# Hybrid encoder on one core: masks moved between the levels, prompt rows loaded a unit sooner, query preparation in two parts, another order at the experts' ends

## Chip, cores and metric

The kernel runs on one core of one Trainium2 chip. The metric is the device time of one execution in microseconds; lower is better.

## What is computed

One encoder layer is applied to two groups with the same weights: a prompt of 512 tokens and a sample of 1024 tokens, each of width 1024. The layer is a mixer (four differential-attention heads and four bidirectional HGRN2 heads of width 128, from one common input projection, then an output projection) and an expert-choice feed-forward (16 experts, each takes the 2/16 of a group's tokens that score highest), with norms ahead of both and at the end. Cut to the core:

```python
def trunk(x):
    x = x + mixer(rms_norm(x, norm_mix_g))
    x = x + expert_choice_ffn(rms_norm(x, norm_ffn_g))
    return rms_norm(x, final_norm_g)

def mixer(h):
    aq, ak, av, hq, hff, hfb, hi, hg = split(h @ w_in)
    att = diff_attention(aq, ak, av, lam)          # softmax(q1 k1) - lam * softmax(q2 k2), distance bias
    att = rms_norm(att, subln_g) * (1 - lam_init)
    o_f = hgrn2_chunk_scan(silu(hq), 1 - f_f, hi, log(f_f))       # forward
    o_b = flip(hgrn2_chunk_scan(flip(...), 1 - f_b, ...))         # backward
    hgo = rms_norm(o_f + o_b, hg_norm_g) * silu(hg)
    return concat(att, hgo) @ w_out

def expert_choice_ffn(h):
    g, idx = top_k(softmax(h @ w_router).T, cap)   # cap: 128 of the sample, 64 of the prompt
    hid = silu(xs @ w_gate) * (xs @ w_up)          # xs = h[idx]
    return scatter_add(idx, (hid @ w_down) * g)
```

## The kernel before, in words

Activations and weights are split into a high and a low part (`w_hi` by a cast on ScalarE, `w_lo` by a subtraction on VectorE), and each product is three matmuls (hi*hi, lo*hi, hi*lo; L599 to L601). Each engine runs its own program; steps are named by tuples, and every engine walks through the same written list of steps. Semaphores (`Signal`, counted by head and number) tie the engines together.

The order of the program is this, with the times of the profiled execution. First the sample's and the prompt's rows are normalised and turned (0 to 30 us). The turned prompt rows go to DRAM and come back later. Then come the sample's four hgrn heads: a first head, a loop, and a last one "joined" with the first projection units of attention (345 to 425). Then the sample's attention heads: three in a loop-like form (425 to 650, the last of them called lone), and the last one, the "crossing" (650 to 727), in whose gaps the first units of the prompt's hgrn head stand. Then the prompt's hgrn heads (730 to 865), its joined head (865 to 910), its attention heads (910 to 1007), the output projection with router and choice of tokens (1007 to 1226), and the experts (1229 to 2143), an ending behind them.

- `Projection` (L510) multiplies input-projection weights of one head with the rows. Its work comes in units, a unit in `CUTS` pieces. VectorE's `split_lo` (L572) makes `w_lo`, ScalarE's `split_hi` (L568) `w_hi`. `summed` counts PE's finished pieces.
- `unpack` (L475) brings the prompt's turned rows back from DRAM in four quarters: SP's load into `hP_raw` (L486), ScalarE's cast into `hP_hi` (L492), VectorE's subtraction into `hP_lo` (L500). The rows of the sample lie in the same memory, so SP waits until the sample's last projection is done.
- `hgrn` (L845) works in blocks of 512 tokens (two for the sample, one for the prompt: 12 blocks in all). In a block each of seven "levels" multiplies decayed queries and keys (VectorE L1130 to L1141, PE L997 to L1008) into the PSUM banks `X[0..3]`. Step `diag` takes from each bank the 12 x 32 numbers of the diagonal with a mask (L1181) and sums the 12 (L1186); GpSimd places the result (L1276). Then follow the state (L1203) and the normalised output (L1216), turned by PE at L1056.
- `attention` (L1293) works in tiles of 128 queries. Scores (L1449, L1450), two custom operations and exponentials (L1581, L1528), the state of weights (L1598), a turn by PE (L1463), the product with v (L1472) and the output. After four tiles the output is normalised (L1620), turned (L1480) and written to `mixT` (L1627, step `mix`). Step `take` prepares the next head's keys and queries: ScalarE L1517 and L1521, VectorE L1568. Turned keys go through ScalarE to `k_rows` (L1535).
- `project_out` (L1649) runs over tiles of 128 tokens; L1815 is the router product, L1822 and L1829 turn its scores.
- The experts work on units of 128 rows of weights; `gather` fetches the chosen rows (GpSimd L2420), `turn` transposes them on PE (L2187, L2188), ScalarE L2251 and VectorE L2326 split them to `x_parts`; `split` is L2244 and L2319 for weights; units are L2210 and L2212. The ending adds the last expert (L2378, L2383, L2390), and normalises and scatters the last rows (L2369, L2460).

## Time and profile before

| | us |
| --- | --- |
| median of three runs | 2164.92 |
| lowest and highest | 2163.8, 2165.94 |
| the profiled execution | 2165.15 |
| its span in the trace | 2162.9 |
| mean granted TensorE clock | 0.973 |

| engine | busy us | share of the span |
| --- | --- | --- |
| PE | 1996.9 | 92% |
| DVE (VectorE) | 1450.8 | 67% |
| ACT (ScalarE) | 1108.7 | 51% |
| POOL (GpSimd) | 352.6 | 16% |

PE is TensorE, PEld its weight load. A wait row names the instruction that waited and the one that released it. The span is shorter than the time of the execution by what lies before the first and behind the last instruction. L numbers are lines of the kernel before; in the changed kernel the same lines stand some 6 to 30 lines further down (L1181 becomes L1193, L2187 becomes L2215).

### The profile page before, as it was taken

What the parts mean: (1) busy time and instruction counts of PE and PEld (TensorE: products, weight loads), DVE (VectorE), ACT (ScalarE), POOL (GpSimd) and SP (SyncE); (2) the same over time, 40 slices, a digit from 0 to 9 for tenths busy, and PEclk for the clock granted to TensorE, in tenths of its full rate; (3) what the DMA queues carried; (4) which work ended last, traced back from release to release, by engine and by line L of the source; (5) the groups of instructions that cost most, each with busy time, mean ns of one, the idle gap of its engine ahead of it and who ended that gap; (6) DMA issues with size and microseconds to landing.
All of it is one profiled execution on the core that took longest, in us unless ns stands there. A gap on an engine that the chain in (4) does not pass through costs nothing. (4 is left out here: it accounts for less than half of the span.)

```text
span 2162.9 us, 43529 instructions
## 1 busy us (share of the span) xinstructions
PE 1996.9 (92%) x16048; PEld 1746.7 (81%) x16048; DVE 1450.8 (67%) x2601; ACT 1108.7 (51%) x1983; POOL 352.6 (16%) x587
## 2 busy tenths in 40 slices
PE   7999998899998998888899199999999999999996
PEld 6877876788787776677788199999999999999995
DVE  5366575666667666676258677777777777778875
ACT  5322322465566433366222066667666766667774
POOL 1213213000000122201221001111111111111233
PEclk9999999999999999999999599999999999999998
DMA  5211100100002222112232278777878887778995
GB/s 183 84 31 32 35 27 17 41 18 24 20 6 88 64 58 82 62 52 80 98 117 100 109 231 265 247 260 247 266 246 260 247 263 248 259 257 297 345 323 189
DMA packets 183465, 317.82 MB, mean 147 GB/s; under 512 B 11872, under 2 KB 82016, under 8 KB 183328
## 3 DMA queue, kind: packets, MB, share of 16 engines
q1 hardware_dynamic: 169984, 281.06, 38.5%
q0 software_dynamic: 8608, 30.68, 5.7%
q10 hardware_dynamic: 4736, 4.19, 0.7%
q8 instruction: 93, 1.52, 0.3%
q14 instruction: 44, 0.36, 0.1%
HBM read 279.97 MB, written 35.91 MB: 146 GB/s over the span
## 5 line engine op out<-in xcount | busy, mean ns | idle before, releaser
L2319 DVE TENSOR_TENSOR we_lo<-raw,we_hi 128x1024 fp32r<-128x1024 f32 x384 | 465.9, 1223 | 189.2 <-ACT we_hi L2244 188.4
L2210 PE MATMUL psum<-x_parts,we_hi 128*128 128x384 f32 x2048 | 585.5, 360 | 3.1 <-DVE we_lo L2319 3.1
L2212 PE MATMUL psum<-x_parts,we_lo 128*128 128x192 f32 x2048 | 513.6, 251 | 0.0
L2244 ACT CAST we_hi<-raw 128x1024 fp32r<-128x1024 f32 x384 | 400.1, 1054 | 157.0 <-PE psum L2212 93.7
L2212 PEld LDWEIGHTS psum<-x_parts,we_lo 128*128 128x128 f32 x2048 | 392.3, 192 | 0.6
L2210 PEld LDWEIGHTS psum<-x_parts,we_hi 128*128 128x128 f32 x2048 | 385.8, 188 | 4.1 <-issue 3.5
L599 PE MATMUL psum<-hT_hi,w_hi 128*128 128x512 f32 x512 | 213.8, 417 | 1.4 <-issue 0.7
L601 PE MATMUL psum<-hT_hi,w_lo 128*128 128x512 f32 x512 | 201.7, 394 | 0.0
L600 PE MATMUL psum<-hT_lo,w_hi 128*128 128x512 f32 x512 | 201.4, 393 | 0.0
L599 PE MATMUL psum<-hP_hi,w_hi 128*128 128x512 f32 x256 | 109.8, 429 | 16.5 <-DVE w_lo L572 12.2
L134 POOL TENSOR_TENSOR carried_pool<-minus_half 128x1 f32<-128x1 f32 x47 | 16.9, 359 | 635.3 <-ACT result_s L2286 489.6
L601 PEld LDWEIGHTS psum<-hT_hi,w_lo 128*128 128x128 f32 x512 | 97.0, 189 | 21.6
L599 PEld LDWEIGHTS psum<-hT_hi,w_hi 128*128 128x128 f32 x512 | 97.0, 189 | 21.1 <-DVE w_lo L572 1.3
L600 PEld LDWEIGHTS psum<-hT_lo,w_hi 128*128 128x128 f32 x512 | 97.3, 190 | 16.3
L572 DVE TENSOR_TENSOR w_lo<-w_raw,w_hi 128x512 fp32r<-128x512 f32 x96 | 68.1, 709 | 56.5 <-ACT w_hi L568 54.8
L600 PE MATMUL psum<-hP_lo,w_hi 128*128 128x512 f32 x256 | 102.3, 400 | 0.0
L601 PE MATMUL psum<-hP_hi,w_lo 128*128 128x512 f32 x256 | 102.0, 398 | 0.0
L2226 PE MATMUL psum<-we_hi,hid_parts 128*128 128x512 f32 x256 | 101.3, 396 | 0.0
L2227 PE MATMUL psum<-we_lo,hid_parts 128*128 128x512 f32 x256 | 99.8, 390 | 0.0
L2228 PE MATMUL psum<-we_hi,hid_parts 128*128 128x512 f32 x256 | 99.7, 390 | 0.0
L2230 PE MATMUL psum<-we_lo,hid_parts 128*128 128x512 f32 x256 | 99.6, 389 | 0.0
L2229 PE MATMUL psum<-we_hi,hid_parts 128*128 128x512 f32 x256 | 99.6, 389 | 0.0
(313 smaller groups left out, 3836.2 us busy)
## 6 DMA issues: line engine op xcount, KB each, us to landing
raw<-in_w_gate SPq DMA_DIRECT2D x128, 512.0 KB, 4.7
raw<-in_w_up SPq DMA_DIRECT2D x128, 512.0 KB, 6.9
raw<-in_w_down SPq DMA_DIRECT2D x128, 512.0 KB, 5.0
w_raw<-in_w_in SPq DMA_DIRECT2D x96, 256.0 KB, 2.8
y_rows<-x SPq DMA_DIRECT2D x12, 512.0 KB, 2.6
h_rows<-h SPq DMA_DIRECT2D x12, 512.0 KB, 2.9
y<-y_rows SPq DMA_DIRECT2D x12, 512.0 KB, 8.0
w_raw_s<-in_w_in SPq DMA_DIRECT2D x16, 256.0 KB, 3.1
```

The source lines that it names most:

```text
L599: pe.matmul(out[:], mem.w_hi[:, u % 2, n, :], hi, start=(k == 0), stop=False)
L600: pe.matmul(out[:], mem.w_hi[:, u % 2, n, :], lo, start=False, stop=False)
L601: mm = pe.matmul(out[:], mem.w_lo[:, u % 2, n, :], hi, start=False, stop=(k == DT - 1))
L2210: pe.matmul(out[:, 0:2 * SLOTS], w_hi[:, s, at], x_parts[p][:, k, :, :], start=(k == 0), stop=False, skip_group_check=True)
L2212: mm = pe.matmul(out[:, SLOTS:2 * SLOTS], w_lo[:, s, at], x_hi[p][:, k, :], start=False, stop=(k == DT - 1), skip_group_check=True)
L2226: pe.matmul(out[2 + h][:], a, u, start=first, stop=False)
L2227: pe.matmul(out[2 + h][:], a, v, start=False, stop=False)
L2228: pe.matmul(out[2 + h][:], b, u, start=False, stop=last)
L2229: pe.matmul(out[h][:], both, u, start=first, stop=False)
L2230: mm = pe.matmul(out[h][:], both, v, start=False, stop=last)
L2244: act.copy(w_hi[:, n % PARTS, :], raw[:, s, :]).then_inc(hi.sem, 1)
L2319: dve.tensor_tensor(w_lo[:, n % PARTS, :], raw[:, n % RAW, :], w_hi[:, n % PARTS, :].bitcast(F32), ALU.subtract).then_inc(lo.sem, 1)
```

## The change

Seven parts:

1. **Masks inside the levels.** `diag` no longer reads the banks. One of the four masks stands behind level 5 and three behind level 6, and they write to rows of 32 with the four banks side by side. `diag` is then four additions over 768, 384, 128 and 128 elements, each on the result of the one before, in place of four reductions.
2. **Prompt rows a unit sooner.** `unpack` waits for attention's next-to-last unit of the last sample head instead of its last. The memory is cut anew, so that the raw rows and the early half don't lie on what the last unit reads. Two quarters are unpacked in the lone head, two in the crossing; only the late half waits for the last unit. PE's own wait at the start of the prompt's hgrn (`start`) is gone.
3. **Queries in two parts.** `take` 0 makes both keys and the first pair of queries, `take` 1 the second pair a tile later.
4. **Output turn a tile later.** `mix` of the first half stands at tile 6 between two pieces instead of behind tile 5.
5. **Dummy matmuls.** PE multiplies `ident` with itself 16 times behind the router product of the next-to-last tile, and 28 times ahead of the experts' first turn.
6. **Experts' start.** The first three weight splits stand ahead of the first turn, and SP lets the gathered rows land before it issues the fourth weight chunk.
7. **Experts' end.** The last expert's prompt rows are added, normalised and scattered ahead of the sample's rows.

```diff
+def keep_clock(pe, bank, ident, count):
+    for _ in range(count):
+        pe.matmul(bank[:, 0:P], ident[:], ident[:], start=True, stop=True)
...
+        {"hP_raw": ([P, DT, TP], F32), "hP_late": ([P, 2, HALF, TP], F32R), "hP_early": ([P, 2, HALF, TP], F32R),
+         "w_raw_p": ([P, 2, HALF, P], F32)},
...
-        sp.wait_ge(before.proj.summed.sem, before.proj.summed.last(HEADS - 1))
+        sp.wait_ge(summed.sem, summed.at(HEADS - 1, before.proj.NB * (before.proj.units - 1) - 1))
...
+            if 2 * q >= HALF:
+                act.wait_ge(summed.sem, summed.last(HEADS - 1))
+            act.copy(half_of(0, q), of(mem.hT_raw, q)).then_inc(hi_done.sem, 1)
...
+    in_lone = {("norm", 1): [step for _, step in unpacked[0:2]]}
...
+    at_step = {("scores", 0, 0): [("h", ("split", 0))], ("exp", 1, 0): unpacked[2:3], ("weigh", 0): unpacked[3:4]}
...
-            elif kind == "start":
-                all_mixed(pe)
...
+        behind_level = {5: (0,), 6: (1, 2, 3)}
...
+                for n in behind_level.get(k, ()):
+                    dve.wait_ge(placed.sem, placed.at(i, 4 * b - 1))
+                    dve.tensor_tensor(mem.masked[:, :, n, :], X[n][:, 0:12 * 32].rearrange("p (k t) -> p k t", t=32),
+                                      mem.masks[:], ALU.mult).then_inc(masked.sem, 1)
...
-                for n in range(BC):
-                    e = BC * b + n
-                    dve.wait_ge(summed_up.sem, summed_up.at(i, e - 2))
-                    dve.tensor_tensor(mem.masked[:, n % 2, :, :], X[n][:, 0:12 * 32].rearrange("p (k t) -> p k t", t=32),
-                                      mem.masks[:], ALU.mult).then_inc(masked.sem, 1)
-                    dve.wait_ge(masked.sem, masked.at(i, e))
-                    if n == 0:
-                        dve.wait_ge(placed.sem, placed.at(i, 4 * b - 1))
-                    dve.tensor_reduce(mem.diag[:, n, :], mem.masked[:, n % 2, :, :].rearrange("p k t -> p t k"),
-                                      AX_X, ALU.add).then_inc(summed_up.sem, 1)
+                dve.wait_ge(masked.sem, masked.at(i, BC * b + BC - 1))
+                for e, (to, of) in enumerate(((slice(0, 6), slice(6, 12)), (slice(0, 3), slice(3, 6)),
+                                              (slice(0, 1), slice(1, 2)), (slice(0, 1), slice(2, 3)))):
+                    dve.wait_ge(summed_up.sem, summed_up.at(i, 4 * b + e - 1))
+                    dve.tensor_tensor(mem.masked[:, to, :, :], mem.masked[:, to, :, :], mem.masked[:, of, :, :],
+                                      ALU.add).then_inc(summed_up.sem, 1)
...
+        if turned_out:
+            slots += [("piece", CUTS * (t + 1)), ("mix", t // BC - 1)]
         if 0 < t < NT:
             slots.append(("weigh", t))
         if t == NT - 1:
-            slots.append(("take",))
-        if t < NT - 2 + NB:
+            slots.append(("take", 0))
+        if turned_out:
+            slots.append(("piece", CUTS * (t + 1) + 1))
+        elif t < NT - 2 + NB:
             slots.append(("pieces", t + 1))
         elif NB == 2:
-            slots.append(("pieces", NT + 1))
+            slots += [("take", 1), ("pieces", NT + 1)]
         else:
-            slots.append(("piece", CUTS * NT + t - NT + 1))
-        if middle:
-            slots.append(("mix", t // BC - 1))
...
+                m = step[1]
+                if m == 0:
+                    act.wait_ge(proj.land_act.sem, proj.land_act.at(j, NB * K + NB - 1))
+                    if i is None:
+                        for held in (before.signals[name] for name in ("mixed", "o_summed", "gates", "gate_taken")):
+                            act.wait_ge(held.sem, held.last(HEADS - 1))
+                    act.wait_ge(scored.sem, scored.last(j - 1))
+                    for of in range(2):
+                        act.copy(k_both[of][rows_of(of), 0:T], mem.land[K][rows_of(of), 0:T]).then_inc(k_first.sem, 1)
+                for half in range(2):
+                    high = act.activation(q_hi[m][rows_of(half), 0:T], mem.land[Q][rows_of(m), 0:T], ACT.Copy,
+                                          scale=slope_cols[rows_of(m), 0, bass.ds(j, 1)])
...
+                if t == NT - 2:
+                    pe.wait_ge(added, 2 * (NT - 1))
+                    keep_clock(pe, SUMS[NT % 2][0], ident, 16)
...
             body("gather", 0, 0)
+            for n in range(PARTS - 1):
+                body("split", 0, 0, n)
             body("turn", 0, 0)
             body("gather", 0, 1)
-            for n in range(PARTS - 1):
-                body("split", 0, 0, n)
...
+                            if p == 0 and n == PARTS - 1:
+                                sp.wait_ge(gathered.sem, gathered.at(0, 31))
...
+                    if kind == "gather":
+                        if p == 0:
+                            keep_clock(pe, half(p, "gate")[0], ident, 28)
+                    elif kind == "turn":
...
+        in_turn = sorted(when, key=lambda q: when[q]) + [NT + 2 * LATE - 1, NT + 2 * LATE - 2]
```

The order of instructions is shown at three places, register instructions left out. VectorE, at the first block of a sample's hgrn head, the last level's operands (`q`, `k`) and the diagonal. Before (L572 weight split, L1181 mask, L1186 sum, L1130 the state's operands):

```order
L1139 TENSOR_TENSOR q1<-q1,fup 128x4x64
L1141 TENSOR_TENSOR k1<-k1,fup 128x4x64
L572 TENSOR_TENSOR w_lo<-w_raw_s,w_hi 128x512
L1181 TENSOR_TENSOR table<-psum,table 128x384
L1186 TENSOR_REDUCE table<-table 128x32
L1181 TENSOR_TENSOR table<-psum,table 128x384
L1186 TENSOR_REDUCE table<-table 128x32
L1181 TENSOR_TENSOR table<-psum,table 128x384
L1186 TENSOR_REDUCE table<-table 128x32
L1181 TENSOR_TENSOR table<-psum,table 128x384
L1186 TENSOR_REDUCE table<-table 128x32
L1130 TENSOR_TENSOR q0<-q0,f10 128x512
```

After (L1193 is the mask, L1201 an addition, L1154 and L1156 the operands, L586 the split):

```order
L1156 TENSOR_TENSOR k1<-k1,fup 128x8x32
L1193 TENSOR_TENSOR table<-psum,table 128x12x32 x3
L1154 TENSOR_TENSOR q0<-q0,fup 128x4x64
L1156 TENSOR_TENSOR k0<-k0,fup 128x4x64
L1154 TENSOR_TENSOR q1<-q1,fup 128x4x64
L1156 TENSOR_TENSOR k1<-k1,fup 128x4x64
L586 TENSOR_TENSOR w_lo<-w_raw_s,w_hi 128x512
L1201 TENSOR_TENSOR table<-table 128x768
L1201 TENSOR_TENSOR table<-table 128x384
L1201 TENSOR_TENSOR table<-table 128x128
L1201 TENSOR_TENSOR table<-table 128x128
L1145 TENSOR_TENSOR q0<-q0,f10 128x512
```

The masks moved ahead of the last level's operands (one stands two pairs of rows further up, behind level 5) and of the weight split; the four reductions are gone and four shorter additions stand behind the split.

ScalarE, at the crossing, from the last `take` of the sample to the first exponentials of its last head. Before:

```order
L1517 CAST k_both<-land 64x1024 x2
L1521 ACTIVATE q_hi<-land,slope_cols 64x1024 x4
L568 CAST w_hi<-w_raw 128x512
L1535 COPY k_rows<-psum 128x512 x2
L1541 ACTIVATE squares,small<-psum 128x128 x4
L1504 COPY land<-psum 128x512 x2
L1528 ACTIVATE q,small<-k,small 128x1024 x2
L1509 COPY v_rows<-psum 128x512 x2
L1528 ACTIVATE f,small<-k,small 128x1024
L492 CAST hP_hi<-hP_raw 128x1024 x2
L568 CAST w_hi<-w_raw 128x512
L492 CAST hP_hi<-hP_raw 128x1024 x2
```

After (L1536 and L1538 are `take`, L582 the weight cast, L1552 k_rows, L506 the prompt rows):

```order
L1536 CAST k_both<-land 64x1024 x2
L1538 ACTIVATE q_hi<-land,slope_cols 64x1024 x2
L582 CAST w_hi<-w_raw 128x512
L1552 COPY k_rows<-psum 128x512 x2
L1538 ACTIVATE q_hi<-land,slope_cols 64x1024 x2
L1558 ACTIVATE squares,small<-psum 128x128 x4
L506 CAST hP_early<-hP_raw 128x1024 x2
L1521 COPY land<-psum 128x512 x2
L582 CAST w_hi<-w_raw 128x512
L1545 ACTIVATE q,small<-k,small 128x1024 x2
L1526 COPY v_rows<-psum 128x512 x2
L1545 ACTIVATE f,small<-k,small 128x1024
L506 CAST hP_late<-hP_raw 128x1024 x2
```

Two of the four query rows moved behind the k_rows copies; the first two casts of prompt rows moved ahead of the copies of the projection, in front of the last head's exponentials.

PE, from the output projection's last product of the sample's second-last tile to the experts' first turn. Before (L1794 product, L1815 router, L1822 and L1829 turns of scores, L2187 and L2188 turns of gathered rows):

```order
L1794 MATMUL psum<-wo,w_lo 128x512
L1815 MATMUL psum<-router,h2T 128x16 x8
L1822 MATMUL psum<-ident,small_o 16x128
L1804 MATMUL psum<-ident,h_1 128x128 x8
L1815 MATMUL psum<-router,h2T 128x16 x8
L1822 MATMUL psum<-ident,small_o 16x128
L1829 MATMUL psum<-ident,merging 128x16 x4
L2187 MATMUL psum<-ident,rows_p 128x128
L2188 MATMUL psum<-ident,rows_s 128x128
```

After (L140 is the dummy, L1814 the product, L1835 the router, L1845 and L1852 the turns of scores, L2215 and L2216 those of rows):

```order
L1814 MATMUL psum<-wo_hi,w_lo 128x512
L1835 MATMUL psum<-router,h2T 128x16 x8
L140 MATMUL psum<-ident 128x128 x16
L1845 MATMUL psum<-ident,small_o 16x128
L1824 MATMUL psum<-ident,h_1 128x128 x8
L1835 MATMUL psum<-router,h2T 128x16 x8
L1845 MATMUL psum<-ident,small_o 16x128
L1852 MATMUL psum<-ident,merging 128x16 x4
L140 MATMUL psum<-ident 128x128 x28
L2215 MATMUL psum<-ident,rows_p 128x128
L2216 MATMUL psum<-ident,rows_s 128x128
```

Sixteen dummies now stand ahead of the wait for the scores, and 28 ahead of the first turn. On ScalarE and VectorE the first three weight splits moved ahead of this turn's copies.

## Rows read from the trace of the kernel before

**Rows 1.** The page's first line; windows (length, busy us of each engine).

```profile
span 2162.9 us, 43529 instructions
...
1246.00:2143.00 897.00, 895.00 (x5552) 843.24 (x5552) 660.34 (x859) 599.37 (x915) 153.32 (x167) 1.00 0.81 266
```

**Rows 2.** PE's waits in the whole span (total us, times, longest).

```profile
PE psum L1829 <- DVE merging L1969: 23.9, 2, 14.1
...
PE psum L599 <- DVE w_lo L572: 12.8, 12, 7.9
...
PE psum L1463 <- DVE mixT L1627: 2.7, 4, 0.7
```

**Rows 3.** The same, 30 to 345 us, then 345 to 425 us.

```profile
PE psum L997 <- DVE table L1181: 4.9, 6, 1.0
...
PE psum L997 <- DVE table L1181: 3.3, 4, 1.1
```

**Rows 4.** Groups by line (ns), then groups of the page.

```profile
L1181 DVE TENSOR_TENSOR table<-psum,table x48: 539/550/559, 113.7 to 891.6; 128x384 f32<-128x384 f32 x48
...
L1186 DVE TENSOR_REDUCE table<-table x48: 803/850/881, 114.3 to 892.2; 128x32 f32<-128x384 f32 x48
...
L2319 DVE TENSOR_TENSOR we_lo<-raw,we_hi 128x1024 fp32r<-128x1024 f32 x384 | 465.9, 1223 | 189.2 <-ACT we_hi L2244 188.4
...
L572 DVE TENSOR_TENSOR w_lo<-w_raw,w_hi 128x512 fp32r<-128x512 f32 x96 | 68.1, 709 | 56.5 <-ACT w_hi L568 54.8
```

**Rows 5.** What PE waited for in 865 to 910 us.

```profile
PE psum L1056 <- DVE normed L1216: 3.3, 1, 3.3
```

**Rows 6.** Timeline, the crossing (start, length, [idle before <-releaser]).

```profile
660.41 1.28 DVE L1598 SCALAR_TENSOR_TENSOR state<-q,small 128x1024 f32<-128x1024 f32 x1
...
663.49 0.79 PE L599 MATMUL psum<-hP_hi,w_hi 128*128 128x512 f32 x1 [7.86 <-DVE w_lo L572]
...
668.13 0.27 PE L1463 MATMUL psum<-ident,state 128*128 128x128 f32 x1
```

**Rows 7.** Timeline at the start of the prompt's hgrn heads.

```profile
730.37 0.49 PE L599 MATMUL psum<-hP_hi,w_hi 128*128 128x512 f32 x1 [1.39 <-DVE mixT L1627]
```

**Rows 8.** PE's waits, 425 to 650, 910 to 1007; timeline, ScalarE.

```profile
PE psum L1472 <- ACT k_rows L1535: 2.7, 3, 0.9
...
PE psum L1472 <- ACT k_rows L1535: 5.4, 3, 1.8
...
PE psum L599 <- DVE w_lo L572: 2.6, 6, 0.6
...
930.36 2.93 ACT L1521 ACTIVATE q_hi_p<-land,slope_cols 64x512 fp32r<-64x512 f32 x4
```

**Rows 9.** Timeline of PE at the router.

```profile
1193.60 0.38 PE L1822 MATMUL psum<-ident,small_o 128*16 128x128 f32 x1 [4.86 <-DVE small_o L1944]
```

**Rows 10.** Timeline, experts' start; DMA view of 1229 to 1243.

```profile
1231.34 0.94 POOL L2420 DMA_INDIRECT rows_s<-h_rows,index_s  x1 [0.30 <-issue]
...
1239.78 0.47 PE L2187 MATMUL psum<-ident,rows_p 128*128 128x128 f32 x1 [13.64 <-DMA rows_s<-h_rows,index_s]
...
1240.04 0.42 PE L2188 MATMUL psum<-ident,rows_s 128*128 128x128 f32 x1
...
1241.67 3.26 DVE L2326 TENSOR_TENSOR x_parts<-psum,x_parts 128x384 fp32r<-128x384 f32 x8 [15.15 <-ACT x_parts L2251]
...
1246.59 0.68 PE L2210 MATMUL psum<-x_parts,we_hi 128*128 128x384 f32 x1 [3.14 <-DVE we_lo L2319]
...
DMA packets 2190, 4.73 MB, mean 338 GB/s; under 512 B 140, under 2 KB 140, under 8 KB 2189
```

**Rows 11.** Windows of PE (busy, clock); sum of four, joined heads.

```profile
1246.59:1251.03 4.44, 4.44 (x17) 0.50 0.79 261
...
sum 20.43, PE 17.21; mean PE 4.30
```

**Rows 12.** Timeline, the last scatter issue.

```profile
2152.65 0.95 POOL L2460 DMA_INDIRECT out_prompt<-late_p,index_cols  x1 [2.10 <-DVE late_p L2369]
```

More of the change, by code:

```diff
@@ L735, in program, with heads @@
         n, h, a, (unpacked,) = bodies
-        def heads(body, steps, units, then=None, lone_steps={}):
+        def heads(body, steps, units, then=None, lone_steps={}, other=tile):
             for lone in (False, True):
@@ L1331, in attention @@
     for t in range(NT + 1):
-        middle = t > BC and t % BC == 1
+        middle, turned_out = (t > BC and t % BC == at for at in (1, 2))
         if t:
@@ L2485, in _ @@
                             body("gather", i + 1, p)
-                for part in range(2):
-                    power(in_turn[part - 2])
-                    put(LATE - 1, (part,))
+                for q in in_turn[-2:]:
+                    power(q)
+                put(LATE - 1, (1, 0))
                 for part in range(2):
```

116 lines of the change are left out of this document (54 added, 62 removed).

## The prediction

> **What bounds the kernel now.** I read the page's first line and the list of PE's waits first, then that list stretch by stretch, then the timeline around the places that the diff touches. The span is 2162.9 us and the program's time in the profiled run was 2165.15, so 2.25 us lie outside the span; the median of three runs is 2164.92, 0.23 below it, which I leave out of the sum. TensorE is the engine that the end waits for: in the experts (1246 to 2143 us) it is busy for 895 of 897 us [rows 1]. Nothing in the diff removes work from it, so the change can only shorten the moments in which PE stands idle. Those lie ahead of the experts, and each has a releaser. The largest, 23.9 us at L1829, is the choice of the tokens and is untouched. The change works at the others: 12.8 us for VectorE's split of a weight chunk (L599<-w_lo), 7.86 of it in one place, and 2.7 us in four places for an output turn's banks (L1463<-mixT) [rows 2].
>
> **Masks (B).** In a block of an hgrn head VectorE ran four masks and four reductions one after the other, 0.55 and 0.85 us each: 5.6 us. PE's next level matmuls write the banks that the masks read, so PE waited 4.9 us in the three looped sample heads, 3.3 us in the sample's last head [rows 3]. Now the masks stand between the levels and four additions of 768, 384, 128 and 128 elements take the place of the reductions. No addition of these shapes is in the trace. The nearest rows are two-input operations of 1024 and 512 elements, 1.22 and 0.71 us [rows 4]: 1.0 ns an element and 0.2 us a start, so 0.97 + 0.58 + 0.33 + 0.33 = 2.2 us. The masks now write rows of 32 with gaps of 96; I take 0.55 for them still (bounds 0.55 and 1.1, twice). A block is 2.2 + 2.2 = 4.4 us of VectorE, 1.2 less. PE's own waits of 4.9 don't all go, because three masks (1.65 us) now stand ahead of the last levels, which PE waits for: I take 3.0 of 4.9 for the looped heads, in the sample's last head 3.5, the 3.3 and a little more, because its levels are paced by VectorE (not all of the 2 x 1.2 us that its two blocks save). The prompt's four blocks save 4.8 us of VectorE; waits behind it there are 3.3 us (the joined head's output turn) [rows 5] and most of 2.3 us for w_lo (12.8 less the 7.86 and less 2.6 in attention, [rows 2, 8]): 2.9 of these 5.6. B together: −9.4, with ends at −4 and −13.
>
> **Prompt rows a unit sooner (A).** PE's idle of 7.86 us ends at 663.49 with w_lo. Before it stand, on ScalarE and VectorE, the casts and subtractions of the unpacked rows. Once the rows are unpacked in the head before, the first prompt unit can start as soon as PE is free, at some 656.3. But the next thing in PE's order is the turn of tile 0's state, which VectorE made from 660.41 to 661.69; it started at 668.13, so it can come sooner by 6.4 us at most [rows 6]. PE will have a new idle of some 3 us between unit and turn, and the later half of the rows (two casts, two subtractions of 1.2 us) still runs there. I take −3.5, ends −1.5 and −5.6. **PE's start of the prompt's first hgrn head** drops its own wait of 1.39 us [rows 7]: the banks are checked by each unit anyway, −1.2 (ends 0 and −1.4).
>
> **Queries in two parts (C).** ScalarE wrote four halves of q_hi in a row, 2.93 us in a prompt head, and the k_rows copy that PE waits for stood behind them. Two of the four now run a tile later, 1.5 us less ahead of the copy. PE's waits for it are 2.7 us in the sample (all shorter than what is taken away, since a sample head's halves are twice as long): −2.7. In the prompt they are 5.4 us in three places, the longest 1.8, and w_lo waits of 2.6 in six places stand beside them; three times 1.5 less is 4.4, and part returns a tile later, where the second half now stands ahead of the squares: −3.3 (ends −1.5 and −5) [rows 8].
>
> **Output turn a tile later (D).** It takes the four bank waits away, 2.7 us [rows 2]; VectorE's copy has a whole piece of PE's work (2.8 us) to hide behind. −2.5, ends −1 and −3.3.
>
> **Clock matmuls in the router (E).** I take a dummy for two passes like a transpose, 0.42 us at half clock (0.21 from one transpose's start to the next [rows 10]) and 0.21 at full. Sixteen fit at full clock into the 4.86 us in which PE waits until 1193.60 [rows 9]; at half they take 6.8 us, and the stage ends behind VectorE's choosing anyway. 0, ends 0 and −0.2.
>
> **Experts' start (F).** The gather of rows_s was issued at 1231.34, but its rows share the queues with eight weight chunks of 0.5 MB: in 1229 to 1243 4.73 MB went at 338 GB/s, and PE's first transpose waited until 1239.78. Now only three chunks and the gathers, 2.6 MB, stand ahead of it. The mean counts the start, in which little flows; without 1.9 us of start it is 391 GB/s (an estimate: 4.73 MB in 12.1 us), and 2.6 MB take 6.7 us from 1230.9: the gather lands at 1237.5 (ends 1235.7 and 1239). From the first transpose to unit 0 went 6.81 us: 1.9 to the first subtraction, 3.26 for eight of them, and then the weight splits, with L2210 waiting 3.14 us for w_lo. The splits now stand ahead of the turn, so 1.9 + 3.26 less 0.3 (the last subtraction's tail) remain, 4.9: unit 0 at 1242.4 instead of 1246.59, −4.2 (ends −1 and −6.5) [rows 10]. The clock: unit 0 ran at half speed until 1251.03, 4.44 us; the 28 dummies should raise it, which would give 2.2 us more if it stayed up. But behind the dummies PE stands idle until the gather lands and then runs only transposes, and after the sixteen transposes of before it was still at half when unit 0 began. I take 0 for the clock [rows 10, 11]. The Trainium skill, "TensorE: Matmul & The Clock Gate", section "Part 4: PE-mode transpose", says that a transpose does not count as PE-busy in the same way as a matmul and that the full clock is not engaged by it; by that rule the clock that the dummies raise would be lost again by unit 0. The sixteen transposes of before agree with it [rows 10, 11].
>
> **Experts' end (G).** Prompt rows now go first, the sample's last. The last scatter was issued at 2152.65 [rows 12]; the same operations in the other order give 2152.5. 0, ends −0.7 and +0.7.
>
> **Sum.** −9.4 −3.5 −1.2 −2.7 −3.3 −2.5 −4.2 = −26.8 us. 2165.15 − 26.8 = 2138.4.
>
> **Rivals.**
> *1. The waits come back.* In the joined heads VectorE paces the levels; a wait that goes at a mask reappears at the next level, for k, q or the state. For it: most of what the change moves stays on VectorE and ScalarE. Against: B takes work from VectorE, it doesn't only move it. Half of the sum: −13.4, 2151.8.
> *2. The 28 dummies are longer than the gather.* At half clock 28 dummies of 0.42 us last 11.8 us and end at 1240.6, later than the rows of before. Then unit 0 starts at 1245.5 and F is −1.1: 2141.5. It is decided by whether PE's clock rises during the dummies; if it does, they end before the gather lands. For it: PE has been idle or transposing at half clock since 1189.6; against: dummies have no gaps at all.
> *3. Half-clock stretches vanish.* The waits that go are those behind which the clock falls. In the four stretches at half speed in the joined heads PE was busy for 17.2 us [rows 11]; were half of them at full speed, 4.3 us, and unit 0's 2.2 with them, −6.5: 2131.9. Against: where waits are only shortened, PE's idle stays idle to the clock.
> *4. Slower.* The masks' gapped writes and the additions' gapped reads run at half VectorE's rate: masks 4 x 1.1, additions 4.4, together 8.8 us where 5.6 stood, +3.2 in each of twelve blocks, 38.4 us, in stretches in which PE waits for VectorE already. B becomes +38.4 while the others give −17.4: 2186.2. It decides from a block of 7.05 us on (5.6 + 17.4 / 12). Against: the masks' input from the banks is unchanged, and at 1.4 ns an element (0.55 us for 384) a mask is already slower than the other rows' slope.
>
> **Chances.** Forecast 0.50, first rival 0.13, second 0.19, third 0.13, fourth 0.05. The forecast's own ends (A 2, B 4, C 2, F 3 us, added as squares some 6) give 2131 to 2144. The range for 8 in 10 takes in the third rival and its spread and reaches to just below the first: 2127 to 2150. A measurement tells about 0.2%, 4.3 us, from no change. All but the fourth rival, and a small part of the first, are beyond it: faster 0.94, same 0.01, slower 0.05.
>
> **What would show it.** In the trace of the changed kernel: the idle before the first hP unit below 3 us and the turn near 663 (A); masks of 0.55 us and additions of 2.2 us together (B; masks over 0.9 us mean the fourth rival); k_rows waits in the prompt below 2.5 us in all (C); no wait for mixT (D); the experts' first transpose some 6 us after the gather's issue, where it was 8.4 (F); dummies of 0.21 us each or of 0.42 (second rival); the experts' 897 us unchanged. The prediction is wrong if the waits for k, q and state in the joined heads grow by what those for the mask lose.

## The result, and the profile after

The changed kernel takes 2152.01 us (median, 2150.83 to 2155.29), the kernel before beside it 2165.43 (2163.80 to 2167.99). The ratio is 0.9935 with a 95% interval of 0.992 to 0.995: 13.4 us less, half of the 26.8 us forecast, and outside the stated range.

The page of the profiled execution (its span is 2.26 us shorter than its time, 2152.86), with what PE waited for in the whole span (total us, times, longest):

```profile
span 2150.6 us, 43727 instructions
...
PE 2009.0 (93%) x16136; PEld 1760.4 (82%) x16136; DVE 1439.9 (67%) x2601; ACT 1109.6 (52%) x1983; POOL 361.3 (17%) x587
...
PE psum L1852 <- DVE merging L1992: 23.9, 2, 14.1
...
PE psum L1497 <- DVE normed L1640: 7.6, 4, 2.3
...
PE psum L1480 <- ACT k_rows L1552: 6.2, 4, 2.0
PE psum L1480 <- DVE state L1618: 5.7, 2, 3.4
...
PE psum L1010 <- DVE q L1145: 4.0, 3, 2.4
...
PE psum L613 <- DVE w_lo L586: 2.0, 4, 0.6
...
PE psum L1489 <- ACT k_rows L1552: 1.0, 3, 0.3
```

The waits for the masks (8.2 us in the two stretches of [rows 3]) and for `mixT` [rows 2] are gone, w_lo fell from 12.8 to 2.0 and k_rows at the product of the weights with v (2.7 and 5.4 in the two stretches of [rows 8]) to 1.0. In their place stand waits that the kernel before hardly had: for `normed`, for the `state` and for `q`.

To see where the 13 us went I cut the program at the same PE instructions in both kernels and divided each stage's length into three: PE's **idle** time, the **clock loss** (half of the time in which PE worked while its granted clock was 0.5), and the rest, which is work at full clock. A stage begins with a PE instruction; idle time belongs to the stage whose instruction ends it. The prompt's attention ends here with its last head's last scores, and what is left of that head stands under the output projection; the first 16 dummies stand in the token stage. Each side is the mean of three profiled executions (the second and third are the runs r1 to r4 below); "forecast" is the prediction's sum for that stage.

| stage (us) | before | changed | difference | idle | clock loss | rest | forecast |
| --- | --- | --- | --- | --- | --- | --- | --- |
| sample's hgrn, first and looped heads | 320.9 | 314.0 | −6.9 | −4.6 | −1.0 | −1.4 | −3.0 |
| sample's joined head | 79.5 | 79.8 | +0.3 | −1.0 | +2.1 | −0.7 | −3.5 |
| sample's attention, three heads | 226.3 | 219.4 | −6.9 | −5.1 | 0 | −1.8 | −4.7 |
| crossing, to the prompt's first level | 84.6 | 87.2 | +2.6 | +0.3 | +1.6 | +0.6 | −5.2 |
| prompt's hgrn, with the joined head | 172.7 | 170.1 | −2.6 | −2.9 | +1.1 | −0.8 | −2.9 |
| prompt's attention | 107.4 | 108.7 | +1.3 | −0.1 | +1.3 | +0.1 | −3.3 |
| output projection | 170.6 | 170.7 | +0.1 | 0 | +0.1 | 0 | 0 |
| choice of tokens, to unit 0 | 60.7 | 58.2 | −2.5 | −12.0 | −1.0 | +10.5 | −4.2 |
| experts | 878.0 | 878.2 | +0.3 | +0.4 | +0.1 | −0.2 | 0 |
| sum | 2100.6 | 2086.3 | −14.3 | −25.1 | +4.3 | +6.5 | −26.8 |

The dummies are work that fills idle time: nearly all of the 12.0 us of idle that left the token stage came back as 10.5 us of the rest. Two stages (the looped hgrn heads and the sample's attention) gained more than forecast, and three that were forecast at −12.0 together (joined head, crossing, prompt's attention) came out at +4.2.

### The profile page after: what moved, and what is told of

Its sections match the earlier page's. It is cut to its first block and busy times, and to the rows that moved or that the text cites. A ratio compares the mean times of both kernels' runs of the same rounds, so it can differ in the third digit from the quotient of the medians.

```text
span 2150.6 us, 43727 instructions
## 1 busy us (share of the span) xinstructions
PE 2009.0 (93%) x16136; PEld 1760.4 (82%) x16136; DVE 1439.9 (67%) x2601; ACT 1109.6 (52%) x1983; POOL 361.3 (17%) x587
## 5 line engine op out<-in xcount | busy, mean ns | idle before, releaser
L586 DVE TENSOR_TENSOR w_lo<-w_raw,w_hi 128x512 fp32r<-128x512 f32 x96 | 68.6, 714 | 59.7 <-ACT w_hi L582 58.5
L582 ACT CAST w_hi<-w_raw 128x512 fp32r<-128x512 f32 x96 | 59.1, 616 | 78.4 <-PE psum L615 75.9
L1091 ACT ACTIVATE land<-psum 128x512 f32<-128x512 f32 x60 | 35.9, 598 | 114.0 <-PE psum L615 113.8
L1489 PEld LDWEIGHTS psum<-v_rows,k_rows 128*128 128x128 f32 x640 | 78.2, 191 | 8.4 <-issue 2.9
```

## The experiments

Each run is compared with the kernel before on the same chip. Executions of one kernel differ by up to 9 us, so a single part of a few microseconds is read from its stage and not from the total.

### The masks: taken out, and alone

The first kernel is the changed one with the old step in place of the new:

```diff
-                for n in behind_level.get(k, ()):
-                    dve.tensor_tensor(mem.masked[:, :, n, :], X[n][:, 0:12 * 32]..., mem.masks[:], ALU.mult)
             elif kind == "diag":
-                (four additions)
+                for n in range(BC):
+                    dve.tensor_tensor(mem.masked2[:, n % 2, :, :], X[n][:, 0:12 * 32]..., mem.masks[:], ALU.mult)
+                    dve.tensor_reduce(mem.diag[:, n, :], mem.masked2[:, n % 2, :, :]..., AX_X, ALU.add)
```

> The changed kernel with the four masks and the four reductions back in the diagonal step. Theory (the waits for the masks were the gain of the looped heads, the prompt's too, but in the sample's joined head the four additions took their place): the looped sample heads get 4.5 to 6 us longer, the prompt's hgrn and joined heads 3 to 5 us, the sample's joined head 1 to 3 us shorter; total 2158 to 2161. Rival (what the masks gave was only a luckier phase of the clock): below 2155.

Measured: 2161.42 us (2157.93 to 2166.33), ratio 0.9979 (0.997 to 0.9989). The looped heads took 320.7 us, 6.7 more than the changed kernel's three profiles; the joined head 77.9, 1.9 less; the prompt's hgrn 172.7, 2.6 more. The theory holds in the looped heads, which lie somewhat above its 4.5 to 6 us, and in the prompt, somewhat below its 3 to 5; the total is just above its range. In the joined head its number came true by luck of the clock: the old masks have 0.5 us more idle there than the changed kernel's mean and 1.0 more of the rest, and 3.4 us less clock loss. So the additions did not make that head slower; they took back part of what the masks' new place gave. Then the masks alone on the kernel before:

> The kernel before with the masks' part of the change alone: masks behind levels 5 and 6, four additions. Theory (the masks are the largest part, as the changed kernel lost 9 us without them, and don't lean on the other parts): 2156 to 2159, of it 6 us in the looped sample heads. Rival (with the other parts missing the prompt's share doesn't appear): 2160 to 2162.

Measured: 2157.6 us (2156.66 to 2158.9), ratio 0.9947 (0.9928 to 0.9965). 5.9 us of it are in the looped heads (315.0 for 320.9), as its theory said. By the medians the masks are worth 8 to 10 us in either company: most of what the change gained.

### The additions behind the next level

In the changed kernel's joined head this stands on VectorE and PE (timeline; start, length, operation, idle before and releaser):

```profile
361.12 2.86 DVE L1201 TENSOR_TENSOR table<-table 128x768 f32<-128x768 f32 x4
...
363.90 1.58 DVE L1145 TENSOR_TENSOR q<-q,f 128x512 f32<-128x512 f32 x2
364.84 0.46 PE L1010 MATMUL psum<-q,k 128*32 128x32 f32 x32 [2.40 <-DVE q L1145]
```

The four additions are ahead of the operand that PE needs next. In place of three waits of 1.0 us for the masks there is one of 2.4. The edit puts a block's additions behind the next block's level 0:

```diff
-        slots += [("level", b, k) for k in range(8)] + [("diag", b)]
+        slots += [("level", b, 0)] + [("diag", b - 1)] * (b > 0) + [("level", b, k) for k in range(1, 8)]
+    slots.append(("diag", NB - 1))
```

> The changed kernel, with the four additions of a sample head's first block behind the next block's level 0. Theory (in the joined head PE waits 2.4 us for q because the additions, 2.9 us, stand ahead of it on VectorE): that wait falls below 0.5 us, the joined head's idle from 12.3 to about 10 us; the looped heads and the prompt stay as they are; 2149 to 2151. Rival (the wait goes to the next level): idle stays above 11.5.

Measured: 2151.21 us (2144.45 to 2152.52). What PE waited for in the joined head:

```profile
PE psum L1011 <- DVE k L1157: 3.8, 8, 1.5
...
PE psum L1011 <- DVE q L1146: 1.2, 2, 0.9
```

The wait for q fell from 4.0 to 1.2, and that for k rose from 2.0 to 3.8 us; the stage's idle is 11.4 us instead of 12.2, not 10. The wait of 2.4 us for q is gone, and a new one of 1.5 us for k stands at the next level, behind the additions in their new place. The theory was right on what PE waited for and wrong on what it is worth: most of the wait moved one level on.

### The queries: in one piece, and the second part at two other places

> The changed kernel with the queries taken in one piece again, in both groups. Theory (in two parts it gains 2.7 us of k_rows waits in the sample and, net of the normed waits, 1 to 1.5 us of idle in the prompt, but costs there two half-clock stretches, 3.4 us): the sample's three attention heads 2.5 us longer than in the changed kernel (222 instead of 219.4 us from the first scores to the last head's), the prompt's 2 us shorter (107 instead of 109 us); total within 1.5 us of the changed kernel. Rival (the parts give what the forecast said in both groups): 5 to 6 us slower, 2157 to 2158.

Measured: 2154.18 us (2152.95 to 2156.81), ratio 0.9936. In the sample's attention the three heads took 224.1 us instead of 219.4: the parts are worth 4.7 us there (forecast 2.7). The other 2.2 us (226.3 before) are left for the output turn a tile later; no run has it alone. In the prompt's attention it took 109.6 us, not 107: the clock fell there without the parts as well. So the parts did not cause that loss, and this half of the theory falls; the total lies between the two expectations. The idle is the better measure there: 11.4 us in one piece, 11.8 in two.

Why the prompt gained nothing is in the waits from 890 to 1000 us. In one piece (this run), and behind the dots in two (the changed kernel):

```profile
PE psum L1489 <- ACT k_rows L1552: 5.4, 3, 1.8
...
PE psum L1497 <- DVE normed L1640: 0.5, 1, 0.5
...
PE psum L1497 <- DVE normed L1640: 6.5, 3, 2.3
...
PE psum L1489 <- ACT k_rows L1552: 1.0, 3, 0.3
```

The 4.4 us that k_rows gave came back as 6.0 us for `normed`. My first idea was that take 1 stood ahead of the squares on ScalarE. So it went behind the step mean:

```diff
-            slots += [("take", 1)] * (t == NT) + [("piece", CUTS * NT + t - NT + 1)]
+            slots.append(("piece", CUTS * NT + t - NT + 1))
-    slots += [(kind, NB - 1) for kind in ("squares", "mean", "norm")]
+    slots += [("squares", NB - 1), ("mean", NB - 1)] + [("take", 1)] * (NB == 1) + [("norm", NB - 1)]
```

> The changed kernel, but in the prompt's attention heads the second part of the queries (take 1) stands behind the step mean instead of ahead of the squares. Theory: in the changed kernel take 1 (ScalarE 1.45 us, VectorE 1.51 us) lies in the chain from the last weights' product to the turn of the normed output, and the 4.4 us that k_rows gave are paid back as 6.5 us of waits for normed in three heads, whose idle also lets the clock fall twice (925, 993 us). Then the normed waits fall from 6.5 to about 3 us, at least one of the two half-clock stretches goes, and the kernel takes 2148 to 2150. Rival: the chain is paced by the squares and GpSimd's power anyway, so the normed waits stay above 5.5 and the time is that of the changed kernel, 2152.

Measured: 2151.89 us (2145.71 to 2155.07), ratio 0.9937. The waits for `normed` rose to 7.5 us where 3 were expected; the theory fell in this form. That no stretch of half clock fell into this stage here need not be the edit's doing: the stage's idle rose, to 12.8 us. The timeline of this run shows what was in the way:

```profile
918.83 1.01 POOL L1660 TENSOR_TENSOR small<-small,minus_half 128x4 f32<-128x4 f32 x1 [35.70 <-DVE small L1632]
...
919.70 1.52 DVE L1586 SCALAR_TENSOR_TENSOR q_lo_p<-land,slope_cols,q_hi_p 64x512 fp32r<-64x512 f32 x2 [1.04 <-ACT q_hi_p L1538]
...
921.63 0.69 DVE L1640 TENSOR_TENSOR normed<-psum,small 128x512 f32<-128x512 f32 x1
...
922.38 0.66 PE L1497 MATMUL psum<-ident,normed 128*128 128x128 f32 x4 [2.48 <-DVE normed L1640]
```

GpSimd's power was done at 919.84, and VectorE worked on take 1's half until 921.2 before it went to the norm. So the next kernel has take 1 behind the norm.

> The changed kernel, with take 1 of the prompt's heads behind the step norm, one step later than in the run with take 1 behind mean, where VectorE's half of it (1.52 us) stood ahead of the norm and three waits for normed of 2.5 us were seen. Theory (VectorE's half of take 1 in front of the norm is what paid the k_rows gain back): the waits for normed fall from 6.5 us to under 3 us in the three heads, the idle of the prompt's attention stage from 11.8 to 8 us or less. Rival (the chain through the squares and GpSimd's power is bound otherwise): idle stays above 10.5. The total depends on the clock as well: 2146 to 2152.

Measured: 2153.19 us (2148.39 to 2156.41), ratio 0.9936. Waits in the same stretch:

```profile
PE psum L1466 <- DVE q_lo_p L1586: 2.8, 3, 1.0
PE psum L1497 <- DVE normed L1640: 2.7, 3, 0.9
```

`normed` is at 2.7 us, as the theory said, but the scores behind it now wait 2.8 for q_lo: idle 10.9 us instead of 11.8, where I expected 8, and the total is above the 2146 to 2152 expected. The 1.5 us of VectorE are ahead of the next head's scores wherever they stand. In a prompt head the program has no tile left behind which they could go; in a sample head, with twice the tiles, it has.

### The crossing: rows late again, and a split behind the state

> The changed kernel with the prompt's rows loaded behind the last unit and unpacked in the crossing, as before. Theory (the earlier rows gave little, because the stretch from the last sample head's first scores to the prompt's first level took 86.4 us where it took 84.7 before: the idle before the first prompt unit went to the turn behind it and to ScalarE's queue): within 1.5 us of the changed kernel, 2151 to 2154. Rival (the rows gave their 3.5 us and something else in the crossing took them): 2155 to 2156.

Measured: 2151.11 us (2148.43 to 2153.30), ratio 0.9928. The crossing took 87.8 us, with the changed kernel's three at 86.4, 87.7 and 87.5. Seven other kernels of this study have the changed kernel's crossing as it is, and over all ten profiles it took 85.8 to 89.0 us. So loading the rows a unit sooner is worth nothing that these runs can tell from zero, and not 3.5 us. The crossing's waits in this run, and behind the dots in the changed kernel:

```profile
PE psum L613 <- DVE w_lo L586: 7.8, 1, 7.8
PE psum L1480 <- DVE state L1618: 2.3, 1, 2.3
...
PE psum L1480 <- DVE state L1618: 5.7, 2, 3.4
PE psum L1480 <- ACT k_rows L1552: 2.0, 1, 2.0
PE psum L1466 <- DVE small L1601: 1.4, 2, 1.2
```

The 7.8 us are gone and 3.4 for the state, 2.0 for k_rows and 1.2 for the exponentials' sums stand in their place. And there is a wait of 2.3 for the state in both kernels which the kernel before lacks. The changed kernel's timeline names its cause:

```profile
699.99 0.69 DVE L586 TENSOR_TENSOR w_lo<-w_raw,w_hi 128x512 fp32r<-128x512 f32 x1 [2.68 <-ACT w_hi L582]
700.60 0.74 DVE L1647 TENSOR_SCALAR mixT<-psum,att_g 128x512 f32<-128x512 f32 x1
...
701.81 1.28 DVE L1618 SCALAR_TENSOR_TENSOR state<-q,small 128x1024 f32<-128x1024 f32 x1
703.15 1.73 PE L1480 MATMUL psum<-ident,state 128*128 128x128 f32 x7 [2.24 <-DVE state L1618]
```

To make room for the output turn, a piece of the projection moved ahead of the step that makes the state. In the crossing that piece begins with a weight split, and VectorE stands 2.68 us for ScalarE's cast while the state waits behind it. The edit gives the split its place behind the state again:

```diff
         if step[0] == "piece":
-            crossing += [("h", s) for s in h_p.proj.piece(step[1] - CUTS)]
+            steps = [("h", s) for s in h_p.proj.piece(step[1] - CUTS)]
+            kept += [s for s in steps if s[1][0] == "split"]
+            crossing += [s for s in steps if s[1][0] != "split"]
         elif step[0] != "pieces":
             crossing.append(("a", step))
+            if step[0] == "weigh":
+                crossing += kept
+                kept = []
```

> The changed kernel, with the weight split of the piece at tile 6 of the crossing behind the step weigh. Theory (the output turn a tile later pulled a piece, and with it a weight split, ahead of tile 6's state on VectorE, which then waits 2.7 us for ScalarE's cast while PE waits 2.24 us for the state): that wait disappears or falls below 0.8 us and the crossing gets 1.5 to 3.5 us shorter, 83 to 85 us. Rival (the copy to mixT is what delays the state): the wait stays above 1.5 us.

Measured: 2149.99 us (2145.92 to 2150.78), ratio 0.9926 (0.9911 to 0.9942). The crossing took 84.9 us, below all ten profiles with the split's old place, and 84.9 again in the kernel with three edits further down. Its idle is 9.6 us, where those ten have 10.6 to 12.0. In its waits the state stands once, with 3.4 us:

```profile
PE psum L1485 <- DVE state L1623: 3.4, 1, 3.4
PE psum L1485 <- ACT k_rows L1557: 3.2, 1, 3.2
```

The cause is confirmed: some 2 us for one split's place (−2.3 against the mean of 87.2, 2.0 of it idle), though the wait for k_rows is 3.2 here and was 2.0 to 3.0 in the changed kernel.

### The experts' start

The changed kernel's timeline:

```profile
1215.91 9.41 PE L140 MATMUL psum<-ident 128*128 128x128 f32 x56 [2.36 <-PEq L121]
...
1218.71 0.94 POOL L2447 DMA_INDIRECT rows_s<-h_rows,index_s  x1 [0.31 <-issue]
...
1227.23 0.33 PE L2215 MATMUL psum<-ident,rows_p 128*128 128x128 f32 x1 [1.91 <-DMA rows_s<-h_rows,index_s]
...
1232.54 0.69 PE L2238 MATMUL psum<-x_parts,we_hi 128*128 128x384 f32 x1 [3.33 <-DVE x_parts L2354]
```

From the gather's issue to the first transpose went 8.52 us, before it was 8.44 [rows 10]. From there to unit 0 went 5.31 instead of 6.81. Three kernels take one part each away: SP's wait, the 28 dummies, and the splits' new place.

```diff
-                            if p == 0 and n == PARTS - 1:
-                                sp.wait_ge(gathered.sem, gathered.at(0, 31))
```

> The changed kernel without SP's wait for the gathered rows ahead of the fourth weight chunk. Theory (the gather takes 8.4 us from its issue whether eight chunks or three share the queues, as the two traces show): the first transpose stays within 0.7 us of its place, the fourth and later chunks come earlier, so unit 0 starts at the same time and the next units don't wait: 2151 to 2152.5. Rival (the fourth to eighth chunks do slow the gather, and something else took the gain): the first transpose is 2 us later, 2154.

Measured: 2153.27 us (2150.19 to 2155.16), ratio 0.9933. The first transpose came 8.06 us after the issue, so the theory is right that the fourth to eighth chunks do not delay the gather. But unit 0 began 14.25 us after the issue, and 6.19 after the first transpose instead of 5.31. What they delay is the third chunk, whose split now stands ahead of the rows' copies. Its cast in the changed kernel, and behind the dots in this one, where the first transpose stood at 1227.23 and 1230.11:

```profile
1227.53 1.05 ACT L2272 CAST we_hi<-raw 128x1024 fp32r<-128x1024 f32 x1 [1.55 <-DMA raw<-in_w_gate]
...
1231.29 1.05 ACT L2270 CAST we_hi<-raw 128x1024 fp32r<-128x1024 f32 x1 [0.65 <-DMA raw<-in_w_gate]
```

In all other kernels with the changed start the path from the first transpose to unit 0 took 5.2 to 5.6 us. SP's wait is thus worth some 0.9 us, by letting the third chunk land sooner and not the rows.

```diff
-                            keep_clock(pe, half(p, "gate")[0], ident, 28)
```

> The changed kernel without the 28 dummy matmuls ahead of the experts' first turn (the 16 at the router stay). Theory (the gather takes the same 8.5 us from its issue, and the dummies' clock reaches the transposes and falls again at unit 0): the transposes run at half clock, 3.4 us instead of 1.7, and unit 0 starts 14.5 to 15.5 us after the gather's issue instead of 13.5 to 13.8; unit 0 runs at half clock either way. Rival (the dummies do nothing that reaches unit 0, since the copies behind the transposes pace it): 13.5 to 13.9 us. In both the total stays within its noise of the changed kernel, 2150 to 2155; the place decides.

Measured: 2152.68 us (2150.28 to 2154.66), ratio 0.9922. The transposes ran at half clock, 0.21 us apart instead of 0.11, and yet unit 0 began 12.92 us after the issue (the first transpose came 7.71 after it) and 5.21 after the first transpose. The theory fell: the dummies reach nothing. In the changed kernel VectorE's third weight split ends at 1229.83 and its eight subtractions behind it at 1232.48, and unit 0 starts at 1232.54: they pace this path.

```diff
             body("gather", 0, 0)
-            for n in range(PARTS - 1):
-                body("split", 0, 0, n)
             body("turn", 0, 0)
             body("gather", 0, 1)
+            for n in range(PARTS - 1):
+                body("split", 0, 0, n)
```

> The changed kernel with the experts' first three weight splits behind the first turn and the second gather again. Theory (the splits ahead of the turn removed the wait for we_lo, but the third chunk lands with the rows, so its split delays the rows' copies by some 0.6 us): unit 0 starts 15 to 16 us after the gather's issue, 1.5 us later than in the changed kernel. Rival (the splits' place is worth nothing): 13.5 to 14.

Measured: 2153.02 us (2151.12 to 2154.97), ratio 0.993. Unit 0 began 13.51 us after the issue, 5.53 after the first transpose. This theory fell as well: the place of the splits alone is worth 0.2 us. The first transpose came 7.5 to 9.6 us after the issue over all 18 profiles of this study, and differs more between executions than between these kernels.

### Is the clock loss the change's doing?

After twelve runs the largest open number was the clock loss. The expectations below name 22.6 us for the first profile of before and 20.9 for the kernel with take 1 behind mean; these left out the half-clock time ahead of the trace's first clock record, and with it they are 24.3 and 23.1. The changed kernel's 31.7 stays. Two more executions of each side were profiled.

> The kernel before once more, for a second profiled execution. If the clock loss is the change's doing, PE's work at half clock costs 21 to 25 us here, as in the first profile (22.6), and 4 to 4.5 us in the sample's joined head. If the first profile was a lucky one, 28 us or more.

> The same once more: 21 to 25 us if the change causes the loss, 28 or more if the first profile was lucky; the idle is 131.5 us within 1 us in both cases.

> The changed kernel once more. If the change causes the clock loss, 29 to 34 us (first profile 31.7), 6 to 8.5 us of it in the sample's joined head. If the first profile was an unlucky one, 20 to 27 us. Idle 105 to 107 us in both.

> The same once more: 29 to 34 us of clock loss if the change causes it, 20 to 27 us if the first profile was unlucky.

| | time | idle | clock loss | joined head | crossing | prompt's attention |
| --- | --- | --- | --- | --- | --- | --- |
| before, first profile | 2165.15 | 131.5 | 24.3 | 4.3 | 1.9 | 0 |
| before, r1 | 2167.77 | 129.4 | 29.7 | 4.1 | 1.8 | 3.2 |
| before, r2 | 2168.34 | 131.1 | 27.9 | 7.5 | 1.6 | 3.1 |
| changed, first profile | 2152.86 | 106.3 | 31.7 | 8.1 | 3.1 | 3.4 |
| changed, r3 | 2154.00 | 104.3 | 34.6 | 7.1 | 3.6 | 5.1 |
| changed, r4 | 2150.60 | 106.2 | 28.5 | 6.9 | 3.5 | 1.7 |

(The last three columns are the clock loss of those stages.) Both readings hold in part. The first profile of before was a lucky one: its program lost 3.7 and 5.4 us more in the other two. The means are 27.3 and 31.6; the ranges overlap, so of these 4.3 us only the crossing's part can be called the change's: 1.6 to 1.9 before, 3.1 to 3.6 changed. There the windows of half clock have moved. In those of before, and behind the dots those of the changed kernel (PE busy, granted clock):

```profile
660.52:667.35 6.83, 3.87 (x9) 0.50 0.41 106
...
652.01:655.42 3.41, 2.82 (x8) 0.50 0.00 0
703.21:706.62 3.41, 3.41 (x13) 0.50 0.00 0
```

Before, 3 of the 6.8 us at half clock were idle anyway. Now PE works through nearly all of them, and the second window opens just behind the new wait of 2.24 us at 703.15. That wait is not needed for the loss: in the kernel with the split behind the state, which lacks it, the second window opens 15 us later in the crossing, and the loss is 3.4 us all the same. Which of the change's edits moved the windows is open.

### Three edits together

> The three edits of this call together on the changed kernel. If their idle times add, 2.3 + 2.2 + 3.8 us less idle than the changed kernel: 2143 to 2146 at the same clock. If the clock takes back what idle gives, 2148 to 2151.

Measured: 2145.86 us (2143.43 to 2148.83, five executions), ratio 0.9905 (0.989 to 0.992) to the kernel before. It has the fastest median of all, 6 us below the changed kernel's; the two intervals touch at 0.992, so it is likely faster than the changed kernel, and how much is not settled. The crossing took 84.9 us (87.2) and the joined head 76.2 (79.8). Of that only 2.4 us are idle; 3.7 are clock loss in the joined head. That is luck as far as the runs show: twelve profiles whose joined head has the change's masks and additions lost 2.5 to 8.5 us there. Over all stages the 8.3 us of idle that the expectation added up were 1.4, and the clock loss of this profile (26.9 us) is 4.7 below the changed kernel's mean. So the median falls into the first expectation's range without its reason.

## Why the prediction was wrong, by its own steps

By the sum of the stages the gain is 12.5 us short of the forecast. Three stages account for more than that: the crossing (−5.2 forecast, +2.6 measured), the prompt's attention (−3.3, +1.3) and the sample's joined head (−3.5, +0.3). In each the wait that was priced did shrink or go, and another wait of the same stage took its place; the sum had put those at nothing or too low.

**B, masks** (−9.4 forecast): −6.9 in the looped heads, +0.3 in the joined head, −2.6 in the prompt, −9.2 in all, and 8 to 10 in the two kernels that test it. That the total came out right is luck, since its places were wrong. In the looped heads all of the 4.9 us of [rows 3] went (I kept 1.9 back for the levels, which don't wait there), and 1.4 us of the rest went along. In the sample's attention it was 1.8 us of the rest beside 5.1 of idle: a stage's gain is larger than the sum of its wait rows, by some 0.2 us a wait; what that is made of is not shown. In the joined head the wait of 3.3 us went and that for q grew from 1.2 to 4.0. This is the prediction's own sign of being wrong, and it came true. Without the clock loss (+2.1) the head still gained 1.7 us. The text said itself that VectorE paces this head and drew the wrong conclusion from it, that the head would gain the most. In the prompt the number is near and the reason was another. Its largest wait, 3.3 us for the joined head's `normed` [rows 5], of which I took a part, did not move; what went are the waits for w_lo (1.7 us there, not my 2.3: 0.6 of the rows that I subtracted from stand in the sample's attention), for the masks and for the state. The prompt's hgrn heads before, and behind the dots changed:

```profile
PE psum L1056 <- DVE normed L1216: 4.8, 4, 3.3
...
PE psum L599 <- DVE w_lo L572: 1.7, 3, 0.7
...
PE psum L1019 <- DVE table L1181: 1.0, 2, 0.6
...
PE psum L1069 <- DVE normed L1231: 4.9, 4, 3.3
...
PE psum L613 <- DVE w_lo L586: 0.4, 1, 0.4
```

The masks kept their 0.55 us (0.547 mean) with gapped writes, and the additions took 0.95, 0.66 and twice 0.36 us in the mean, 2.3 together for my 2.2; the fourth rival was far from deciding. These are means of two cases: in the first blocks of the sample's heads, where GpSimd works at the same time, the 384 elements took 0.85 us and a block's four additions 2.87 with the steps between them; in the other blocks GpSimd was idle, and they took 0.56 and 2.19.

```profile
L1193 DVE TENSOR_TENSOR table<-psum,table 128x384 f32<-128x384 f32 x48 | 24.3, 547 | 0.0
...
L1201 DVE TENSOR_TENSOR table<-table 128x768 f32<-128x768 f32 x12 | 11.4, 949 | 0.0
```

**A, prompt rows** (−3.5), with **PE's start** (−1.2) and the crossing's share of **D** (−0.5): +2.6. This is the step that failed most, by 7.8 us. I bounded the gain by the state of [rows 6], and the wait for that state did come, with 3.4 us. I didn't follow the two engines that the rows were moved on: the late half's casts put k_rows back by 2.0 to 3.2 us, and the early half the exponentials by 1.2. And I gave the output turn's move a price of zero beyond its own copy, without looking at what else the moved piece carries: one weight split, some 2 us. The clock loss, 1.6 us more in this stage, was in no term either.

**C, queries**: −4.7 in the sample for −2.7 forecast: against the kernel with the queries in one piece the idle fell by 3.3 us (k_rows 2.6, w_lo 0.6) and the rest by 1.4. In the prompt the idle fell by 0.1 for 3.3 forecast. "Part returns a tile later" was the right mechanism at the wrong size: all of it returned, since at both of the other places tried the 1.5 us of VectorE came out as a wait, for `normed` or for the next scores' q_lo.

**D, output turn**: −2.2 in the sample's three heads for −2.0 forecast there, by difference.

**F, experts' start** (−4.2): −2.5 by stage. The path behind the first transpose shrank by 1.5 where I had 1.9. Of these 1.5, the kernels that take one part away find 0.9 in SP's wait and 0.2 in the splits' place; the rest has no run of its own. The landing was the wrong term: I expected 6.2 us from issue with three weight chunks in the queues instead of eight, and it was 8.5, as before; in the means of three it was 8.8 before and 8.0 changed, with single ones from 7.6 to 9.6, and that is 0.8 of the stage's 2.5. Bytes ahead in the queues, at the bandwidth of [rows 10], did not set it. What does is not settled here. The clock came out as taken, at zero. The dummies raised it at 1222.03, and it fell again as unit 0 began (windows; PE busy, granted clock):

```profile
1222.03:1232.27 10.24, 5.26 (x45) 1.00 0.71 261
1232.27:1235.69 3.42, 3.15 (x11) 0.50 1.06 397
```

That is what the rule of the Trainium skill ("TensorE: Matmul & The Clock Gate", section "Part 4: PE-mode transpose") had said of the transposes. Here the idle before them and behind them (1.91 and 3.33 us) may have done it as well; no run tells the two apart.

**E and G** were put at zero and are near it: from the start of the token stage, in which the 16 dummies stand, to the gather's issue went 45.1 us before and 44.9 now, and from the last expert unit to the end 38.6 and 38.1.

**The clock** was in the forecast only as a gain (third rival). It was a loss, 4.3 us in the means, of which only the crossing's 1.6 are shown to be the change's.

**The rivals.** The first, "the waits come back", had 2151.8 us and a chance of 0.13; the measured time is 2152.01. That the number fits so well is luck, since it is half of the sum and worked out from nothing else. Its argument named the joined heads; it held in the sample's, and in the crossing and the prompt's attention. I gave it too little because I summed most removed waits stage by stage near full value, and looked for what is late next only by name. The second rival fell: the clock rose during the 28 dummies, which ended at 1225.32, ahead of the first transpose at 1227.23.

## What to carry to other kernels

Where the engine that releases a wait goes on to PE's next operand without a gap, as VectorE did in the joined head, most of a removed wait can come back at that operand; follow the next two consumers on that engine before pricing it. When a piece of work is moved, list every instruction that it carries, on each queue: one weight split cost some 2 us here, as much as the move had brought. Compare kernels by stage and by idle time, from several profiled executions: single profiles of one program differed here by up to 6 us of clock.

## What the runs showed of the hardware

The same program with the same waits at the same distances is granted a different clock from execution to execution. The prompt's attention of the kernel before had no half-clock stretch in one profile and lost 3.2 and 3.1 us in two others, with the idle at 12.5, 11.3 and 12.0 us. All stages together, PE's work at full clock agreed within 0.6 us in the three profiles and the idle within 2.2, while the clock loss went from 24.3 to 29.7: most of what single executions differ by is the clock.
